# A mixture-of-experts layer on one core: one table of expert sums in HBM, the last two experts' rows placed in PSUM by one-hot matmuls, and the final norm in the expert loop's block

## The reference

```python
def moe_ffn(h, w_router, b_router, w_gate, w_up, w_down, ws_gate, ws_up, ws_down):
    ...
    def body(y, args):
        tok_b, g_b, e_b = args
        xb = hf[tok_b]
        u = jax.nn.silu(xb @ w_gate[e_b]) * (xb @ w_up[e_b])
        yb = (u @ w_down[e_b]) * g_b[:, None]
        return y.at[tok_b].add(yb), None
    ...
    shared = (jax.nn.silu(hf @ ws_gate) * (hf @ ws_up)) @ ws_down
    return (routed + shared).reshape(B, S, D)
```

## Time and profile before

| | |
|---|---|
| median of 3 runs | 1175.33 us (1174.09 to 1177.63) |
| profiled execution, its own time | 1177.27 us |
| its span, first to last instruction | 1175.5 us |
| TensorE matmuls busy | 1031.5 us (88%) |
| VectorE busy | 834.2 us (71%) |
| ScalarE busy | 519.2 us (44%) |
| GpSimd busy | 305.2 us (26%) |
| DMA | 302.87 MB, mean 258 GB/s |

### The profile page before, as it was taken

The page is one execution under the profiler, slowest core; times in us unless marked ns, Lnnn a source line. Parts: engine busy times, 40 slices in busy tenths (PEclk is TensorE's granted clock), DMA queues, the critical chain, the costliest instruction groups (busy, mean ns, idle before and its releaser), DMA issues. The chain is left out here.

```text
span 1175.5 us, 16031 instructions
## 1 busy us (share of the span) xinstructions
PE 1031.5 (88%) x4777; PEld 733.2 (62%) x4778; DVE 834.2 (71%) x1470; ACT 519.2 (44%) x609; POOL 305.2 (26%) x152
## 2 busy tenths in 40 slices
PE   1899998588699979999999999999999998989950
PEld 1898897257246636776666666666676665656630
DVE  4877899766454666887888777777777777766735
ACT  3334462264021125555555544545554544544512
POOL 0000000000000042554654532432443342323312
PEclk9899998789898989999999999999999999999985
DMA  9775200400935269999999999999999999999843
GB/s 362 251 265 163 74 1 1 180 19 1 367 108 215 108 223 350 348 372 326 336 355 348 348 349 321 354 336 317 349 340 325 325 341 306 338 319 322 289 110 147
DMA packets 84486, 302.87 MB, mean 258 GB/s; under 512 B 10999, under 2 KB 23331, under 8 KB 74925
## 3 DMA queue, kind: packets, MB, share of 16 engines
q1 hardware_dynamic: 70340, 263.31, 62.1%
q0 software_dynamic: 12544, 35.70, 13.2%
q10 hardware_dynamic: 1514, 2.97, 0.7%
HBM read 276.80 MB, written 27.30 MB: 259 GB/s over the span
## 5 line engine op out<-in xcount | busy, mean ns | idle before, releaser
L1786 DVE TENSOR_TENSOR w_gate_up_lo<-side,w_gate_up_hi 128x2048 fp32r<-128x2048 f32 x64 | 146.7, 2294 | 84.4 <-ACT w_gate_up_hi L1703 76.6
L1786 DVE TENSOR_TENSOR w_gate_up_lo<-main,w_gate_up_hi 128x2048 fp32r<-128x2048 f32 x64 | 146.6, 2290 | 81.8 <-ACT w_gate_up_hi L1703 78.8
L1703 ACT ACTIVATE w_gate_up_hi<-side 128x2048 fp32r<-128x2048 f32 x64 | 122.2, 1910 | 128.9 <-DMA side<-in_w_exp_up 93.2
L1703 ACT ACTIVATE w_gate_up_hi<-main 128x2048 fp32r<-128x2048 f32 x64 | 122.3, 1910 | 119.7 <-DMA main<-in_w_exp_up 88.8
L1546 POOL DMA_INDIRECT xg<-h_rows,row_numbers x48 | 115.6, 2408 | 185.5 <-issue 168.0
L1867 PE MATMUL ps<-w_gate_up_hi,xT_hi 128*128 128x512 f32 x512 | 144.9, 405 | 18.4 <-DVE xT_lo L1790 16.7
L1867 PE MATMUL ps<-w_gate_up_hi,xT_lo 128*128 128x512 f32 x512 | 138.3, 392 | 0.0
L1867 PE MATMUL ps<-w_gate_up_lo,xT_hi 128*128 128x512 f32 x512 | 137.6, 391 | 0.0
L1867 PEld LDWEIGHTS ps<-w_gate_up_hi,xT_hi 128*128 128x128 f32 x512 | 91.5, 189 | 40.5 <-issue 24.1
L1867 PEld LDWEIGHTS ps<-w_gate_up_hi,xT_lo 128*128 128x128 f32 x512 | 96.7, 189 | 21.3
L1867 PEld LDWEIGHTS ps<-w_gate_up_lo,xT_hi 128*128 128x128 f32 x512 | 96.6, 189 | 20.9
(11 more groups left out here) (298 smaller groups left out, 1674.4 us busy)
## 6 DMA issues: line engine op xcount, KB each, us to landing
side<-in_w_exp_gate SPq DMA_DIRECT2D x60, 512.0 KB
side<-in_w_exp_up SPq DMA_DIRECT2D x60, 512.0 KB
main<-in_w_exp_gate SPq DMA_DIRECT2D x60, 512.0 KB
main<-in_w_exp_up SPq DMA_DIRECT2D x60, 512.0 KB
side<-in_w_ada SPq DMA_DIRECT2D x20, 1024.0 KB, 7.7
side<-in_w_exp_down SPq DMA_DIRECT2D x16, 1024.0 KB
main<-in_w_exp_down SPq DMA_DIRECT2D x16, 1024.0 KB
maskb<-in_w_exp_down SPq DMA_DIRECT2D x16, 1024.0 KB
```

Source lines behind the costliest of these rows:

```text
L1703: nc.scalar.activation(whi[:, half], wgu[n % RING][:, :, HALF * half:HALF * (half + 1), :] .rearrange("p m c f -> p c m f"), ACT.Copy).the ...
L1786: nc.vector.tensor_tensor(wlo[:, half], src, whi[:, half].bitcast(F32), ALU.subtract).then_inc(s_wlo, 1)
```

## The change

It does five things:

- One table `y_rows` instead of two. It begins with the shared expert's output, and the zero tiles, their waits and one table's pad rows go.
- The add of expert e waits for the landing of e-1's (`SC0 + 16 * e`). The evictions of e still wait for e-2's. Only experts 0 to 61 are added this way.
- Experts 62 and 63 stay in `yb`. VectorE makes one-hot matrices from their token numbers (`place_rows`), and after its last down product TensorE multiplies: for each of the four token tiles, 2 experts x 2 halves, in f32, accumulated in two PSUM banks. `place` lies in `xg[0]`.
- The overflow block and `stage_final` move into the loop's block: each engine, behind its last expert, loads the overflow count, branches, and goes on. SyncE fetches the table once, into `main`, when the add of 61 has landed.
- In the final norm VectorE adds PSUM and the fetched tile, and does the last add for all four tiles; GpSimd does none. ScalarE takes one root of a constant before the first square.

```diff
-            return pool.indirect_dma_start(out=G.y_sums[slot], out_offset=bass.IndirectOffsetOnAxis(ap=sidx[0:rows, n:n + 1], axis=0),
+            return pool.indirect_dma_start(out=G.y_sums, out_offset=bass.IndirectOffsetOnAxis(ap=sidx[0:rows, n:n + 1], axis=0),
                                            in_=yb[0:rows, slot, :], in_offset=None, compute_op=ALU.add)
...
-            s_sc = [isem("scattered_even"), isem("scattered_odd")]
+            s_sc = isem("scattered")
             SC0 = 2 * 16
-            s_yz = isem("y_zero_tile")
-            s_yzd = isem("y_odd_zeroed")
+            SCATTERED = E_N - 2
...
+            LAST_BANK = [0, 6, 2, 4]
+            place = xg[0].rearrange("p (n t) -> p n t", n=2)
...
+            def extra_tiles(eng, body, adds=False):
+                total = eng.value_load(G.extra_tab[0:1, P:P + 1], min_val=0, max_val=MAX_EXTRA)
+                with eng.If(total > 0):
+                    eng.wait_ge(s_dn, E_N)
+                    eng.wait_ge(s_ya, E_N + 1)
+                    eng.wait_ge(s_yd, E_N + 1)
+                    eng.wait_ge(s_place, 2)
+                    eng.wait_ge(s_sc, SC0 + 16 * SCATTERED)
+                    with eng.Fori(0, MAX_EXTRA) as j:
+                        with eng.If(total > j):
+                            body(j)
+                    if adds:
+                        eng.sem_inc(x_done, 1)
+                    else:
+                        eng.wait_ge(x_done, 1)
...
-                sp.wait_ge(s_yz, 1)
-                for i in range(NT):
-                    sp.dma_start(G.y_sums[1][i * P:(i + 1) * P, :], yb[:, 1, :]).then_inc(s_yzd, 16)
...
-                sp.wait_ge(s_wlo, 2 * (E_N - 2))
-                sp.wait_ge(s_sc[0], SC0 + 16 * (E_N // 2))
+                sp.sem_inc(x_dn, 1)
+                def extra(j):
+                    sp.wait_ge(x_dn, j + 1)
+                    e = expert_of(sp, j)
+                    load_gate_up(sp, e, 0, x_wgu)
+                    load_down(sp, e, 0, x_wd)
+                extra_tiles(sp, extra)
+                sp.wait_ge(s_wlo, 2 * (E_N - 1))
+                sp.wait_ge(s_sc, SC0 + 16 * SCATTERED)
                 for i in range(NT):
-                    sp.dma_start(G.y_even[:, i, :], G.y_sums[0][i * P:(i + 1) * P, :]).then_inc(G.s_y_even[i], 16)
+                    sp.dma_start(y[:, i, :], G.y_sums[i * P:(i + 1) * P, :]).then_inc(s_in[i], 16)
+                for i in range(NT):
+                    sp.wait_ge(s_o[i], 1)
+                    sp.dma_start(G.out[0, i * P:(i + 1) * P, :], xt[:, i, :]).then_inc(s_out, 16)
+                sp.wait_ge(s_out, 16 * NT)
...
-                nc.gpsimd.memset(yb[:, 1, :], 0.0).then_inc(s_yz, 1)
                 for n in range(RING - 1):
                     nc.gpsimd.memset(xg[n], 0.0).then_inc(s_zero, 1)
                 for n in range(2):
-                    for p in range(2):
-                        pool.dma_start(G.y_sums[p][SEQ + n * 64:SEQ + (n + 1) * 64, :], G.xt[0:64, 0, :]).then_inc(s_sc[p], 16)
+                    pool.dma_start(G.y_sums[SEQ + n * 64:SEQ + (n + 1) * 64, :], G.xt[0:64, 0, :]).then_inc(s_sc, 16)
...
-                pool.wait_ge(s_yzd, 16 * NT)
...
-                    pool.wait_ge(s_ya, e + 2)
-                    pool.wait_ge(s_yd, e + 2)
-                    pool.wait_ge(s_sc[n % 2], SC0 + 16 * (UNROLL // 2 * t + n // 2))
+                    if ahead(2):
+                        pool.wait_ge(s_ya, e + 2)
+                        pool.wait_ge(s_yd, e + 2)
+                        pool.wait_ge(s_sc, SC0 + 16 * e)
+                        pool.sem_inc(s_passed, 1)
+                        count = count_of(e)
+                        by_size(count, SIZES, lambda rows: add_rows(pool, n % 2, n, rows).then_inc(s_sc, 16))
+                turns(pool, step)
+                pool.sem_inc(x_added, 1)
...
-                    act.wait_ge(s_sc[n % 2], SC0 + 16 * (UNROLL // 2 * t + n // 2))
+                    act.wait_ge(s_sc, 16 * e + (SC0 - 16))
...
-                act.wait_ge(s_yzd, 16 * NT)
...
+                extra_tiles(act, extra)
+                nc.scalar.activation(rt[:, NT:NT + 1], k[:, K_ONES:K_ONES + 1], ACT.Sqrt)
+                for i in range(NT):
+                    act.wait_ge(s_sum, i + 1)
+                    nc.scalar.activation(sq[:, i % 2, :], y[:, i, :], ACT.Square, accum_out=ss[:, i:i + 1]).then_inc(s_sq, 1)
+                    act.wait_ge(s_ms, i + 1)
+                    nc.scalar.activation(rt[:, i:i + 1], ss[:, i:i + 1], ACT.Sqrt).then_inc(s_rt, 1)
...
+                    if not ahead(2):
+                        place_rows(n)
                     dve.wait_ge(s_dn, e + 1)
-                    dve.wait_ge(s_sc[n % 2], SC0 + 16 * (UNROLL // 2 * t + n // 2))
+                    dve.wait_ge(s_sc, 16 * e + (SC0 - 16))
...
+                def place_rows(n):
+                    for i in range(NT):
+                        ins = nc.vector.tensor_scalar(place[:, n % 2, i * P:(i + 1) * P], k[0:CAP, K_IOTA:K_IOTA + P], float(i * P + 1),
+                                                      found[:, n, 0:1], ALU.add, ALU.is_equal)
+                    ins.then_inc(s_place, 1)
                 turns(dve, step)
...
+                extra_tiles(dve, extra)
+                last = Chain(dve, s_last)
+                def add_sums(i):
+                    dve.wait_ge(s_in[i], 16)
+                    dve.wait_ge(s_acc, i + 1)
+                    b = LAST_BANK[i]
+                    nc.vector.tensor_tensor(y[:, i, :], ps[:, b:b + 2, :].rearrange("p a b -> p (a b)"), y[:, i, :], ALU.add).then_inc(s_sum, 1)
+                add_sums(0)
+                for i in range(NT):
+                    if i + 1 < NT:
+                        add_sums(i + 1)
+                    dve.wait_ge(s_sq, i + 1)
+                    nc.vector.tensor_scalar(ss[:, i:i + 1], ss[:, i:i + 1], 1.0 / D, EPS, ALU.mult, ALU.add).then_inc(s_ms, 1)
+                    dve.wait_ge(s_rt, i + 1)
+                    last(nc.vector.reciprocal(rt[:, i:i + 1], rt[:, i:i + 1]))
+                    last(nc.vector.scalar_tensor_tensor(y[:, i, :], y[:, i, :], rt[:, i:i + 1], G.rows[:, 3, :], ALU.mult, ALU.mult))
+                    nc.vector.tensor_tensor(xt[:, i, :], xt[:, i, :], y[:, i, :], ALU.add).then_inc(s_o[i], 1)
...
+                extra_tiles(pe, extra)
+                pe.wait_ge(s_place, 2)
+                pe.wait_ge(s_uTd, E_N + 1)
+                for i in range(NT):
+                    for n in range(2):
+                        pe.wait_ge(s_ya, E_N + n)
+                        pe.wait_ge(s_yd, E_N + n)
+                        for half in range(2):
+                            ins = nc.tensor.matmul(ps[:, LAST_BANK[i] + half, :], place[:, n, i * P:(i + 1) * P],
+                                                   yb[:, n, 512 * half:512 * (half + 1)], start=n == 0, stop=n == 1)
+                    ins.then_inc(s_acc, 1)
...
-        G.y_sums = [nc.dram_tensor(f"y_rows_{name}", (SEQ + P, D), F32, kind="Internal").ap() for name in ("even", "odd")]
+        G.y_sums = nc.dram_tensor("y_rows", (SEQ + P, D), F32, kind="Internal").ap()
```

More of the change, by code:

```diff
@@ L1681, in step, with extra @@
                         by_size(count, SIZES, lambda rows: gather_rows(pool, n % RING, (n + AHEAD) % UNROLL, rows).then_inc(s_g[n % RING], 16))
-                    pool.wait_ge(s_ya, e + 2)
-                    pool.wait_ge(s_yd, e + 2)
-                    pool.wait_ge(s_sc[n % 2], SC0 + 16 * (UNROLL // 2 * t + n // 2))
-                    pool.sem_inc(s_passed, 1)
-                    count = count_of(e)
-                    by_size(count, SIZES, lambda rows: add_rows(pool, n % 2, n, rows).then_inc(s_sc[n % 2], 16))
-                turns(pool, step)
-                for p in range(2):
-                    pool.wait_ge(s_sc[p], SC0 + 16 * (E_N // 2))
+                    if ahead(2):
[7 more added lines that the diff above has]
+                pool.sem_inc(x_added, 1)
+                def extra(j):
+                    pool.wait_ge(x_idx, j + 1)
+                    pool.sem_inc(s_passed, 1)
+                    gather_rows(pool, 1, 0).then_inc(x_g, 16)
+                    pool.wait_ge(x_ya, j + 1)
+                    pool.wait_ge(x_yd, j + 1)
+                    pool.sem_inc(s_passed, 1)
+                    pool.indirect_dma_start(out=G.y_sums, out_offset=bass.IndirectOffsetOnAxis(ap=sidx[:, 0:1], axis=0),
+                                            in_=xyb, in_offset=None, compute_op=ALU.add).then_inc(x_sc, 16)
+                    pool.wait_ge(x_sc, 16 * j + 16)
+                    pool.sem_inc(x_added, 1)
+                extra_tiles(pool, extra, adds=True)
             @block.scalar
@@ L2052, in body @@
+                    pe.wait_ge(x_wd, 16 * j + 16)
+                    pe.wait_ge(x_u, j + 1)
                     for half in range(2):
                         for f in range(FC):
[L2054 removed]
```

(9 more changed lines are left out.)

223 lines of the change are left out of this document (61 added, 162 removed).

## The result

| | before | after |
|---|---|---|
| device time, median | 1175.64 us (4 runs, 1174.09 to 1177.63) | 1156.21 us (4 runs, 1154.33 to 1159.15) |
| profiled execution | 1177.27 us, span 1175.5 | 1159.15 us, span 1157.4 |
| TensorE's last down product to the end of the span | 40.4 us | 25.9 us |

The ratio is 0.9829, with an interval of 0.9811 to 0.9846. The forecast was 1156.6 us; faster was right, and so was the size.

What follows compares the result with a forecast made beforehand. TensorE bounds the loop's first third, the weights' stream the rest, then an end with TensorE idle. End 13.7 plus start 5.0 gives 18.7 us off: 1158.6 for the profiled execution, 1156.6 us forecast against the median, range 1150.5 to 1166.0.

Steps and rivals of the forecast that it cites:

- The end, 13.7 us: After TensorE's last down product: early fetch, placement matmuls and VectorE's norm bring the span to 1161.8 us, 13.7 us less.
- the table load: Final norm: ScalarE's 1.28 us load of its table for the root, hidden behind the wait for the placement.
- The start, 5.0 us: Loop's start: dropping the zero tiles' 2.10 MB and their waits gains 5.0 us, bounds 0.8 and 6.0 + 0.8.
- its two parts: Loop's start: TensorE's next group comes 0.8 us earlier; the weights' stream is spared 2.10 MB, 6.0 us at 350 GB/s.
- It lands some 5 us after its issue ... Cost nothing: Expert loop: each serial add lands some 5 us after issue, the next due over 10 us later, so costs nothing.
- All three signs of being wrong that name the adds: Expert loop: GpSimd's adds waiting for a landing at each expert, a period over 10.82 us, evictions waiting for a DMA.
- The first rival: Expert loop: serial adds set the pace, slower if landing exceeds 9.4 us; at 10 us costs 54 us, 1210 us; 5%.
- The hidden zeros: Loop's start: rival that the zeros were hidden anyway, so only 13.7 + 0.8 us gained, 1160.8 us; chance 26%.
- The stream's larger gain: Loop: rival that a fuller ring delays the DMA-bound regime, gaining 10 us at this place, 1151.6 us; chance 12%.
- The clock: Placement: rival that TensorE's clock falls, doubling the 14.4 us so the end gives nothing, 1171.0 us; chance 4%.
- The two scalings beside GpSimd: Final norm: two scalings took 2.76 instead of 1.29 us beside GpSimd's adds; 2 x 1.47 saved, two 1.23 us adds come.

Runs made afterwards that it cites:

- group 1: Changed kernel again (1156.26 us); with adds into two tables (1156.03); with zeros back, one table (1160.28); with zeros and two tables (1161.04); kernel before 1176.04.
- group 2: Changed kernel with 2.10 MB (1159.34 us) or 4.19 MB (1162.01) of unawaited stores; all 64 experts scattered (1163.86); final norm reordered (1153.03); kernel before 1179.31.
- no placement: Changed kernel with all 64 experts' rows scattered by adds and no placement matmuls, the final stage otherwise the same: 1163.86 us, 0.9878 of the kernel before.
- group 3: Changed kernel again (1153.75 us); with 2.10 MB of unawaited stores (1156.02); norm reordered (1152.35); first two residual adds on GpSimd (1153.39); kernel before 1176.65.

## Why the prediction was right, and where it was not

**The end, 13.7 us: right, 14.6 in the trace** (40.4 - 25.9), 15.0 by the medians of group 1. By its own terms: TensorE's second tile came 6.8 us after the last down product where 7.2 stood (32 passes in 13.90 us are 0.43 us each, not 0.45), and from TensorE's second tile to VectorE's end 16.0 us where 16.5 stood. The whole placement ends 13.7 us after the last down product, forecast 14.5. The fetch, the table load, the one-hot rows and the overflow count were hidden as said: SyncE issues at 1127.31, TensorE pauses nowhere. What the sum doesn't tell is how it divides: without the placement 5.9 us (group 2), with it 8.6 more.

**The start, 5.0 us: right in size, its two parts less sure.** Removing the zeros with their waits is worth 4.0 us with serial adds and 5.0 with two tables, each uncertain by some 3 us. In the traces TensorE reaches the third expert's group at 458.76 instead of 461.09, of which 1.0 us was there before the loop, so 1.3 us where I had 0.8: the idle time before it is gone entirely. The reason given, that 2.1 MB leave a stream which has no air, fits in direction only; the bytes alone measured 0, 2.3 and 2.7 us.

**"It lands some 5 us after its issue ... Cost nothing": the price was right, the reason was wrong, and that they met is luck.** The 80 packets of 487 to 491 us were read as those of the add of 486.80. By the order on the queue they are the gather's, issued before it (GpSimd, the view of the earlier trace rows):

```profile
481.35 2.86 POOL L1546 DMA_INDIRECT xg<-h_rows,row_numbers  x1 [1.37 <-issue]
```

In the trace of after a group of 80 at the same place is the gather's, and the add's comes some 4.5 us after its issue and ends with its landing. For the add of 486.80 itself no wait shows the landing. Under the stream of after an add lands 6.6 to 11.6 us after its issue. The period of a serial chain was to be 1.7 us plus the landing; at the median of 8.5 that is 10.2 us, but 10 of the 27 links make it over 10.82, and the adds of 549 to 790 us came 10.94 us apart in the mean. All three signs of being wrong that name the adds appeared: adds waiting for a landing, a period over 10.82 us in a long stretch, and evictions that wait for a DMA. A fourth effect had not been priced at all: the gather held up behind the add stopped TensorE for 5.3 us and lowered its clock.

The first rival priced these waits as if each lengthened the loop, and group 1 shows none of that: what a late add costs comes back as a shorter wait for weights. Part of this was within reach: the earlier trace rows show the DMA engines as full from 450 us on as they are later, while TensorE never waits there, so the weights must still have been ahead. A wait in that stretch spends this lead, not the end. That full DMA engines are the reason why both loops end together is argued from these rows; no run lightened the stream to see the adds set the end.

The rule of the Trainium skill that the prediction set beside it ("DMA: Bandwidth & Descriptors", Queues, rings and completion order), that an engine goes round robin between its queues, was taken to mean that a backlog of weights would not hold an add up. The prediction saw the add in the loop agree with that; it doesn't. Without weights in flight adds land in 4.6 and 5.1 us (no placement, above), under the stream in 8.5. Part of the difference can be the gather ahead on the same queue; but the last add of the kernel before has no gather ahead, only the fetch beside it, and took 9.3 us.

**The other rivals.** The hidden zeros (1160.8) lie outside the result's interval, and group 1 speaks against them. The stream's larger gain wanted 10 us where the forecast had 5.0; the medians of the three times it was measured (19.4, 19.8 and 22.9 us off) leave 4.8, 5.2 and 8.3 beyond the end's 14.6, so two of three are at the forecast and the last is nearer to the rival. The clock did not fall in the placement, where TensorE had no pause; it fell in the loop, after the wait for the gather.

**The two scalings beside GpSimd.** The prediction set 2 x 1.47 us saved against two adds of 1.23 and so made GpSimd's leaving a small gain. In the new tail it costs 1.4 us (group 3); the sum's total hid this.

## What to carry to other kernels

When one resource sets a total (here the weights' stream) and another the pace of a stretch, price a new wait by whether it spends slack that the first resource gives back, not by how often it shows among the waits or in the chain that ended last. The time from a transfer's issue to its release is read from who waits for it. Packets in a window carry no name: check that the first of them doesn't come before the issue, and look for what stood ahead on the same queue. A tail is compared from its last common event to the end of the span: that told 1.4 and 2.4 us apart, where medians of five runs did not.

## What the runs showed of the hardware

- An accumulating row scatter of 80 to 96 packets releases its waiter 6.6 to 11.6 us after its issue while the weights stream at 330 to 347 GB/s (27 links, 480 to 800 us), and 4.6 and 5.1 us after it when no weights are in flight (no placement). At the add of 505.78 us its packets came behind those of the gather ahead of it on the same queue.
- One wait of 5.3 us in the loop lowered TensorE's granted clock to 0.61 in the mean of 645 to 650 us: a transposition took 1.98 instead of 1.14 us and a down product 5.00 instead of 3.60.
- GpSimd's add and VectorE's scaling slow each other while they overlap. In the kernel before, GpSimd's add ran from 1159.35 to 1162.60 and the scaling began at 1160.93: 1.67 us of overlap, 1.47 us longer than the 1.29 of one alone. In the new tail they overlap by 0.30 and 0.38 us and the scaling is 0.10 and 0.18 us longer. VectorE's sum kept its 1.22 us beside GpSimd in both, but GpSimd's add took 3.25 us when a sum of two SBUF tiles had begun just before it (below, kernel before) and 2.36 beside the sum that reads a matmul's result. Which of VectorE's two instructions lengthened it is not separated.

```profile
1159.18 1.22 DVE L2114 TENSOR_TENSOR main<-main,side 128x1024 f32<-128x1024 f32 x1
```

- The length of the loop varies from one execution to the next: in three traces of the changed kernel, from expert 1's first product to the last down product's start, 679.4, 672.8 and 671.8 us, while the tail agrees to 0.1 us.
